# Order and release of expert weight loads, place of a tile's shares, and fifteen constant products in a mixture-of-experts stage

## The reference, cut to what matters

```
hf = rmsnorm(x)                                   # 1056 x 1024
group = argmax(hf @ wg + bg)                      # 1 of 4 groups
top 2 of the group's 4 experts; gate = softmax(their logits) * p_group
for e in range(16):
    he = silu(hf @ w_gate[e]) * (hf @ w_up[e])    # 1024 -> 512
    y += combine[:, e] * (he @ w_down[e])         # 512 -> 1024
```

## Time and profile before

| | us |
|---|---|
| median of 3 runs | 1438.02 (1435.93 to 1444.21) |
| the profiled execution, whole | 1435.85 |
| its span, first to last instruction | 1433.6 |
| part of the span ahead of the mixture | 0 to 928 |
| routing and the first tiles' start | 928 to 1000.4 |
| first to thirteenth `yo` | 1000.4 to 1257.8 |
| the rest of the tiles, until the last `yo` | 1257.8 to about 1409 |
| last scatter and the copy of the outputs | to 1433.6 |

### The profile page before, as it was taken

One profiled execution on the slowest core, in us unless ns is written; L12 is line 12 of the kernel. 1 busy time (PEld: TensorE's weight loads), 2 busy tenths in 40 slices (PEclk: granted clock), 3 DMA queues, 4 the chain that ended last, 5 costly groups with the idle time before them and its releaser, 6 DMA issues. The chain is left out here.

```text
span 1433.6 us, 20022 instructions
## 1 busy us (share of the span) xinstructions
PE 1144.5 (80%) x6603; PEld 944.8 (66%) x6603; DVE 870.5 (61%) x1294; ACT 576.2 (40%) x858; POOL 207.1 (14%) x217
## 2 busy tenths in 40 slices
PE   0799998696465788888885998639998979799992
PEld 0679998594252355566564998538777857688881
DVE  0740699485887454445532424457877867699990
ACT  2221211224412232222333002217777767588881
POOL 3021222003400100000000000001212232232211
PEclk9999999798595587777976999759999989899996
DMA  5301111101100255443417103386996989777415
GB/s 147 92 30 45 45 45 44 45 4 27 31 3 16 82 149 179 140 122 96 122 33 235 49 1 147 121 356 225 343 385 195 332 322 346 284 230 236 118 30 150
DMA packets 92073, 200.82 MB, mean 140 GB/s; under 512 B 17675, under 2 KB 75376, under 8 KB 85756
## 3 DMA queue, kind: packets, MB, share of 16 engines
q1 hardware_dynamic: 81228, 164.51, 32.3%
q0 software_dynamic: 8064, 29.04, 8.3%
q10 hardware_dynamic: 2704, 6.29, 1.3%
HBM read 175.69 MB, written 28.74 MB: 143 GB/s over the span
## 5 line engine op out<-in xcount | busy, mean ns | idle before, releaser
L2004 DVE TENSOR_TENSOR w_lo<-raw_gu,w_hi 128x1024 fp32r<-128x1024 f32 x176 | 205.2, 1220 | 73.6 <-ACT w_hi L1837 70.4
L1837 ACT CAST w_hi<-raw_gu 128x1024 fp32r (+1 forms) x176 | 178.2, 1051 | 57.1 <-PE ps L2064 30.7
L2064 PE MATMUL ps<-w_hi,hg_hi 128*128 128x512 f32 x352 | 145.1, 412 | 33.5 <-DVE w_lo L2004 31.0
L2064 PE MATMUL ps<-w_lo,hg_hi 128*128 128x512 f32 x352 | 141.7, 403 | 0.0
L2064 PE MATMUL ps<-w_hi,hg_lo 128*128 128x512 f32 x352 | 141.5, 402 | 0.0
L199 PE MATMUL ps<-hT_hi,wz_hi 128*128 128x352 f32 x384 | 128.0, 333 | 0.0
L199 PE MATMUL ps<-hT_lo,wz_hi 128*128 128x352 f32 x384 | 124.6, 325 | 0.0
L199 PE MATMUL ps<-hT_hi,wz_lo 128*128 128x352 f32 x384 | 124.6, 324 | 0.0
L2004 DVE TENSOR_TENSOR w_lo<-raw_d,w_hi 128x1024 fp32r<-128x1024 f32 x88 | 104.7, 1222 | 4.9 <-ACT w_hi L1837 2.5
L2064 PEld LDWEIGHTS ps<-w_hi,hg_hi 128*128 128x128 f32 x352 | 69.2, 197 | 51.1 <-DVE w_lo L2004 30.4
L1837 ACT CAST w_hi<-raw_d 128x1024 fp32r (+1 forms) x88 | 91.0, 1053 | 19.8 <-PE ps L2064 19.3
(11 more groups left out here) (423 smaller groups left out, 2406.2 us busy)
## 6 DMA issues: line engine op xcount, KB each, us to landing
raw_gu<-in_exp_w_gate SPq DMA_DIRECT2D x16, 2048.0 KB, 12.7
raw_gu<-in_exp_w_up SPq DMA_DIRECT2D x16, 2048.0 KB, 18.0
raw_d<-in_exp_w_down SPq DMA_DIRECT2D x16, 2048.0 KB, 9.0
kpg<-in_cache_k SPq DMA_DIRECT2D x128, 128.0 KB, 2.0
vpg<-in_cache_v SPq DMA_DIRECT2D x128, 128.0 KB, 2.5
wz<-in_w_in SPq DMA_DIRECT2D x16, 512.0 KB, 4.1
wo<-in_w_out SPq DMA_DIRECT2D x4, 1024.0 KB, 8.4
x<-in_x_prompt SPq DMA_DIRECT2D x8, 512.0 KB, 10.6
```

The lines of the kernel that those rows point to most:

```text
L1837: e.copy(to, raw).then_inc(hi_done, 1)
L2004: e.tensor_tensor(w_lo[:, slot_, :], raw, w_hi[:, slot_, :].bitcast(F32), ALU.subtract).then_inc(lo_done, 1)
L2064: i = e.matmul(out, a, b[:, w, cols], start=(first and n == 0), stop=(last and n == 2))
```

## The change

Three edits, all in `mixture`.

SP: the first two experts' gate and up are issued ahead of their downs. From expert 2 on, gate x waits for `lo_done` of 12 t + 4, up x for 12 t + 8 (t the last tile of expert x-2), and then comes down of expert x-1, which waits for 12 t' + 20 (t' the last tile of expert x-3).

POOL: in `scatter`, `next_share` stands right after the wait for `y_a`, ahead of the wait for the scatter before and of the tile's own scatter. The drains are where they were with their copies.

PE: products of a constant (`ident` with 512 columns of `reset`, f32) into a free PSUM bank: three ahead of the counting products, six behind them, six behind the table's.

```diff
-                def load(x, gu_after=None, d_after=None):
...
+                def load_gu(x, after=None):
+                    for g, of in enumerate((m.exp_w_gate, m.exp_w_up)):
+                        if after is not None:
+                            e.wait_ge(lo_done, after + KE * g)
+                        e.dma_start(raw_gu[:, x % 2, KE * g:KE * g + KE, :].rearrange("p u n -> p (u n)"),
+                                    of[0, x].rearrange("(p k) n -> p (k n)", k=KC)).then_inc(gu_in[x % 2], 16)
+
+                def load_d(x, after=None):
+                    if after is not None:
+                        e.wait_ge(lo_done, after)
...
+                def last_of(x):
+                    return 3 * KE * e.value_load(m.last_tile[0:1, x:x + 1], min_val=0, max_val=S - 1)
+
+                for x in range(2):
+                    load_gu(x)
+                for x in range(2):
+                    load_d(x)
                 e.wait_ge(plan, 1)
-                for x in range(2, NE):
-                    tile = e.value_load(m.last_tile[0:1, x - 2:x - 1], min_val=0, max_val=S - 1)
-                    load(x, 3 * KE * tile + 2 * KE, 3 * KE * tile + 5 * KE)
+                for x in range(2, NE + 1):
+                    if x < NE:
+                        load_gu(x, last_of(x - 2) + KE)
+                    if x > 2:
+                        load_d(x - 1, last_of(x - 3) + 5 * KE)
...
                 def scatter(s, b, before, last=False):
                     e.wait_ge(y_a, s + 1)
+                    if not last:
+                        next_share(s + 1, 1 - b)
                     if before is not None:
                         e.wait_ge(y_sent[1 - b], 16 * before)
                     e.tensor_copy(dcol[b][:], m.table[:, ds(s, 1), 0])
                     e.drain()
...
-                    if not last:
-                        next_share(s + 1, 1 - b)
...
+                def warm(n):
+                    for _ in range(n):
+                        e.matmul(ps[:, 3, :], m.ident[:], m.reset[:, 0:512], start=True, stop=True)
+
+                warm(3)
                 e.wait_ge(oh_done, 1)
...
                 i.then_inc(cnt_mm, 1)
+                warm(6)
                 for t in range(NT):
...
                 i.then_inc(rows_mm, 1)
+                warm(6)
```

More of the change, by code:

```diff
@@ L1764, in _ @@
-                load(0)
-                load(1)
-                e.wait_ge(plan, 1)
-                for x in range(2, NE):
-                    tile = e.value_load(m.last_tile[0:1, x - 2:x - 1], min_val=0, max_val=S - 1)
-                    load(x, 3 * KE * tile + 2 * KE, 3 * KE * tile + 5 * KE)
+                def load_gu(x, after=None):
[4 more added lines that the diff above has]
+                                    of[0, x].rearrange("(p k) n -> p (k n)", k=KC)).then_inc(gu_in[x % 2], 16)
@@ new lines, in load_d @@
+                def load_d(x, after=None):
+                    if after is not None:
+                        e.wait_ge(lo_done, after)
+                    e.dma_start(raw_d[:, x % 2].rearrange("p u n -> p (u n)"),
+                                m.exp_w_down[0, x].rearrange("(p k) n -> p (k n)", k=KE)).then_inc(dn_in[x % 2], 16)
+                def last_of(x):
+                    return 3 * KE * e.value_load(m.last_tile[0:1, x:x + 1], min_val=0, max_val=S - 1)
+                for x in range(2):
+                    load_gu(x)
```

## The result

The changed kernel takes 1426.52 us (median of 4 runs, 1423.52 to 1428.16) against 1438.03 of the kernel before beside it: a ratio of 0.9918, 95% interval 0.9893 to 0.9943. Faster by 0.8%, and 0.5 us from the forecast of 1426. The sum came out right. Of the terms for the three edits only that of the shares did, as the experiments show.

What follows compares the result with a forecast made beforehand. POOL's serial list of gathers, drains and scatters was taken to bound tiles 2 to 12. Start 2.0 less 1.1, plus 10.6 for the share and zero for the queue, gave 11.5 us: 1426, range 1404 to 1440.

Steps and rivals of the forecast that it cites:

- The sum: Whole kernel: start 2.0, first scatter 0.9 earlier, lead of the share 10.6; together 11.5 us, giving 1426.
- The bound: Mixture, tiles 2 to 12: POOL's serial transfers bound, 22.3 us a round against PE's 17.72; load waits lie under them.
- the 44.9 us: Tiles 0 to 12: time lost against PE's pace, 257.5 us against 212.6; all that the first two edits can win.
- two runs of tiles: Sign of being right: in the changed trace `yo` waits for the moved copy's drain, at a gather's end, in two stretches.
- The shares: POOL: `s_ready` given one scatter earlier, a lead given once; `yo` of tile 12 10.6 us earlier, rounds no shorter.
- the new cost: POOL, ahead of the first scatter: no gather hides the moved copy and its drain, about 1.1 us lost.
- The queue: SP: gate and up ahead of down, gate released 5.9 us earlier; worth zero, since ACT's wait lies under POOL's list.
- The constant products: PE, routing: raised clock makes the table 2.7 us earlier, the first gather lands 1.5 earlier, transposes gain 0.5.
- The 0.5 for the transposes: PE, transposes behind the first gather: worth up to 1.0 us if the high clock holds until them; 0.5 taken.
- Loads as the bound: Rival, mixture: weight loads bound at 18.6 us a tile with its own expert; 35.5 us won, time 1400; chance 0.14.
- Slower, loads close the holes: Rival, POOL: loads run beside all eleven rounds, 24.8 us each; 16 us slower, 1454; chance 0.10.
- Low clock: Rival, routing: clock stays low throughout, table 4.6 us late, first scatter 7.5 late; 1435, no change; chance 0.10.

Runs made afterwards that it cites:

- the small loads: Share and queue edits without constant products, drains kept; weight loads of experts 2 and up fetch a sixteenth of their bytes: 1393.5 us, ratio 0.9709 against the kernel before.

## Why the prediction was right, and where it was not

**The bound** was right. POOL's serial list held tiles 2 to 12; taking its drains away returned the whole of the 44.9 us once the new queue was there, and 20.6 with the old one (tile 12 at 302.3 in place of 322.9), where the loads bind next, at rounds of 19.7. That the waits for loads lie under the list holds in that sense. The drain of the moved copy is waited for in tiles 3, 4, 6, 8 and 11, as foreseen, though not in two runs of tiles.

**The shares** were right: 9.4 of 9.5 us at tile 12 with rounds unchanged, 10.0 at the end of the stage (498.7 against 1429.3 - 940.66). Two details differ. The share that comes last is that of tile 11, which waits 8.05 us, and tile 12 follows it at 17.79; the working had tile 12 wait for its own. And the new cost between the first `yo` and the first scatter is 0.4 us (2.78 in place of 2.40), not 1.1.

**The queue** was wrong. The step that failed: "ACT's wait for up lies under the POOL list, where it is worth nothing by itself: zero", taken as zero beside the share too. Alone it is zero (1.0000). But the text names "a gain if POOL's rounds were shorter" as a bound and gives it no price, and has rounds that stay at 22 to 23 us as a sign of being right. With the share they fell to 21.4 to 21.9, and the queue is worth some 9 us there. Why the gain is kept behind the share and lost without it is not shown; what the trace has is that without the share `yo` goes on waiting for POOL up to tile 16. Together the two are some 15 us, not 10.6 + 0 - 1.1.

**The constant products** were wrong: 2.0 forecast, nothing measured. The clock did rise and the table came 3.6 us earlier, 2.7 forecast. What failed is "The weights on the queue are the same, so I take 1.5 us earlier", of a landing "between 959.2 and, at the loop's 11.8 us beside loads, 963.8". The earlier gather runs beside more of the first weight loads and takes 10.4 us where it took 7.2: before, the DMA share had fallen to 0.28 from 960 to 962, ahead of the transposes; in the changed kernel it is 1.02 until they start. The products alone show the same, 10.6 us (955.55 to 966.13). The 0.5 for the transposes failed as well; the stretches of the last six products, of the idle time behind them and of the transposes (the sixth number after the window, ahead of the DMA share and GB/s, is the granted clock):

```profile
957.40:962.80 5.40, 5.40 (x13) 2.20 (x12) 4.49 (x18) 0.00 (x0) 1.79 (x3) 1.00 1.00 428
963.00:969.90 6.90, 0.00 (x0) 0.00 (x0) 3.17 (x3) 0.00 (x0) 0.00 (x0) 0.81 1.02 427
969.90:972.00 2.10, 1.97 (x8) 1.57 (x8) 0.00 (x0) 0.05 (x1) 1.19 (x2) 0.50 0.99 421
```

PE was at 2.4 GHz, stood idle until the gather landed, and did the transposes at 1.2, in the same 1.97 us as before. The Trainium skill, TensorE: Matmul & The Clock Gate, section What's actually happening, has idleness bring the low clock back; the trace agrees: 0.50 in the last stretch.

**The sum.** The queue's missing 4 to 12 us and the products' surplus 2 offset in part, and the changed kernel measured twice is 11.5 and 15.6 us below the one before. That the forecast came within 0.5 us is to that extent luck.

**The rivals.** *Loads as the bound* did not come: rounds were 21.4. Without drains, where it could have come, tiles keep to 17.7 rather than 18.6. The stretches of that kernel (last number: GB/s):

```profile
1030.00:1220.00 190.00, 190.00 (x905) 159.85 (x904) 177.69 (x173) 163.87 (x194) 53.73 (x75) 1.00 0.97 371
1040.00:1058.00 18.00, 18.00 (x87) 15.15 (x86) 16.83 (x17) 15.54 (x19) 5.46 (x7) 1.00 1.01 403
```

At 403 GB/s 17.7 us move 7.1 MB of the 7.3 that a tile with its own expert needs, an estimate; the loads would fall only a little behind, and tiles of an expert already loaded let them catch up. The Trainium skill, DMA: Bandwidth & Descriptors, section Specifications, gives an HBM limit of about 358 GB/s for a core; on this core, which runs alone, 371 over 190 us lie above it. *Slower, loads close the holes* did not come: rounds got shorter, not longer, though the small loads confirm that loads draw rounds out: without them rounds are at PE's 17.7. *Low clock* did not come.

## What to carry to other kernels

A large wait names the engine that stands, not the work that bounds: giving the share early won one lead and then a wait elsewhere, while letting the list overlap its own transfers won 27 us more. Where two edits free two waits on one path, price them in order, the second on the trace that the first leaves; alone, the second may read as zero, as the queue did here. Before paying for an earlier start of a transfer, look at what else is moving at that moment.

## What the runs showed of the hardware

A drain on POOL that only has to cover a small copy (some take 0.2 us) stood as long as the transfer in front was on its way: in the changed kernel's loop for 3 to 13 us, and 0.8 where none was under way; the count on the copy costs about 1 us (1047.18 to 1048.17, both copies of a scatter among it). With a gather and a scatter under way at once beside the loads each is slower (scatters 11.8 us in the median against 6.9), and yet the tiles lose nothing. Rates went to 428 GB/s in the stretch ahead of the transposes. And two profiles of one code differ by 6 us in the last tiles alone, by where a gather meets the last loads, as far as I can see; differences of that size between single profiles mean nothing.
